# Diagonal scores as column sums of an elementwise product, taken second in the order of the levels

## What is computed

```
g_f = log_forget(h_ff, lb_f); g_b = log_forget(h_fb, lb_b)
k_f = -expm1(g_f); k_b = -expm1(g_b)
out_f = chunk_scan(q, k_f, g_f, v)
out_b = chunk_scan(q[:, ::-1], k_b[:, ::-1], g_b[:, ::-1], v[:, ::-1])[:, ::-1]
o = rmsnorm(out_f + out_b, norm_gain)
...
# inside chunk_scan: b = cumsum(g)
scores = einsum('bhtk,bhsk,bhtsk->bhts', q, k, exp(b_t - b_s))   # s <= t
```

## Time and profile before

| | |
|---|---|
| median of 3 runs | 1738.81 us (1738.01 to 1739.43) |
| the profiled execution's own time | 1739.63 us |
| its span, first to last instruction | 1737.8 us |
| TensorE matmuls busy | 1725.9 us (99%) |
| VectorE busy | 1252.2 us (72%) |
| ScalarE busy | 998.8 us (57%) |
| GpSimd busy | 59.3 us (3%) |
| granted TensorE clock, mean | 0.999 of full |
| moved by DMA | 311.65 MB, 179 GB/s |

### The profile page before, as it was taken

One profiled execution on the slowest core, in us unless ns is written; L12 is line 12 of the kernel. 1 busy time (PEld: TensorE's weight loads), 2 busy tenths in 40 slices (PEclk: granted clock), 3 DMA queues, 4 the chain that ended last, 5 costly groups with the idle time before them and its releaser, 6 DMA issues.

```text
span 1737.8 us, 24185 instructions
## 1 busy us (share of the span) xinstructions
PE 1725.9 (99%) x9517; PEld 1498.4 (86%) x9517; DVE 1252.2 (72%) x1584; ACT 998.8 (57%) x1247; POOL 59.3 (3%) x95
## 2 busy tenths in 40 slices
PE   9999999999999999999999999999999999999998
PEld 8888998888888888888889888888888988888887
DVE  6766777766677566875667898866657898876565
ACT  6544666644467454754457866464446966565454
POOL 7200000000000000000001000000000000000000
PEclk9999999999999999999999999999999999999999
DMA  7765535665655655465545554356565554445652
GB/s 244 240 194 185 177 122 169 217 216 180 206 169 176 206 186 188 141 199 192 193 147 191 186 167 145 122 185 218 178 209 169 164 176 134 138 165 194 200 187 96
DMA packets 211564, 311.65 MB, mean 179 GB/s; under 512 B 6434, under 2 KB 166112, under 8 KB 211360
## 3 DMA queue, kind: packets, MB, share of 16 engines
q1 hardware_dynamic: 207472, 303.84, 53.4%
q0 software_dynamic: 3712, 6.44, 1.3%
q10 hardware_dynamic: 304, 0.33, 0.1%
HBM read 309.54 MB, written 1.05 MB: 179 GB/s over the span
## 4 chain that ended last, share of the span: by engine, by line
PE 90%; ACT 5%; DVE 3%; issue 2%; DMA 0%; SPq 0%; ACTq 0%; DVEq 0%
PE psD L1968 28%; PE psA L1905 20%; PE psA L1912 11%; PE psA L1826 7%; PE psA L1831 3%; PE psA L1935 3%; PE psA L1950 3%; PE psA L1770 3%; PE psA L1968 2%; PE psD L2253 2%; ACT hi L454 2%; PE psA L1954 1%; PE psA L1939 1%; PE psA L1775 1%; PE psA L2038 1%
## 5 line engine op out<-in xcount | busy, mean ns | idle before, releaser
L926 DVE TENSOR_TENSOR lo<-raw,hi 128x2048 fp32r<-128x2048 f32 x285 | 650.6, 2290 | 120.1 <-ACT hi L454 119.4
L454 ACT ACTIVATE hi<-raw 128x2048 fp32r<-128x2048 f32 x285 | 542.9, 1911 | 62.2 <-PE psD L1968 33.5
L1905 PE MATMUL psA<-xT,hi 128*128 128x512 f32 x1536 | 355.9, 389 | 0.0
L1905 PEld LDWEIGHTS psA<-xT,hi 128*128 128x128 f32 x1536 | 288.3, 188 | 59.8
L1968 PE MATMUL psD<-hi,prod_hi 128*128 128x512 f32 x544 | 213.5, 392 | 0.2 <-DVE prod_lo L1303 0.2
L1968 PE MATMUL psD<-hi,prod_lo 128*128 128x512 f32 x544 | 212.6, 391 | 0.0
L592 ACT ACTIVATE scr<-psA 128x512 f32<-128x512 f32 x66 | 39.4, 597 | 296.5 <-PE psA L1912 278.7
L1912 PEld LDWEIGHTS psA<-xT,lo 128*128 128x128 f32 x1536 | 190.6, 192 | 3.7
L1912 PE MATMUL psA<-xT,lo 128*128 128x256 f32 x1536 | 191.8, 283 | 0.0
L1284 DVE TENSOR_TENSOR scr<-psA,scr 128x512 f32<-128x512 f32 x66 | 45.6, 691 | 192.2 <-ACT scr L592 192.2
L1968 PE MATMUL psD<-lo,prod_hi 128*128 128x512 f32 x544 | 143.6, 389 | 0.0
(11 more groups left out here) (311 smaller groups left out, 2155.4 us busy)
## 6 DMA issues: line engine op xcount, KB each, us to landing
raw<-in_w_in SPq DMA_DIRECT2D x48, 1024.0 KB, 5.2
raw<-in_ffn_w_up SPq DMA_DIRECT2D x43, 1024.0 KB, 5.7
raw<-in_ffn_w_gate SPq DMA_DIRECT2D x43, 1024.0 KB, 5.4
raw<-in_ffn_w_down SPq DMA_DIRECT2D x43, 1024.0 KB, 5.0
raw<-in_w_gate SPq DMA_DIRECT2D x22, 1024.0 KB, 5.4
raw<-in_w_up SPq DMA_DIRECT2D x22, 1024.0 KB, 5.6
raw<-in_w_down SPq DMA_DIRECT2D x22, 1024.0 KB, 5.0
raw<-in_lru_w_in SPq DMA_DIRECT2D x10, 1024.0 KB, 5.4
```

The source lines that it names most:

```text
L454: act.activation(hi[:, n % RING, :], raw_of(n), ACT.Copy).then_inc(hi_ready, 1)
L926: dve.tensor_tensor(lo[:, n % RING, :], raw_of(n), hi[:, n % RING, :].bitcast(F32), ALU.subtract).then_inc(lo_ready, 1)
L1905: pe.matmul(psA[:, bank + f, :], w[:, k, f * P:(f + 1) * P], xT[:, k].rearrange("p e s -> p (e s)"), start=(k == 0), stop=False)
```

## The change

The diagonal is no longer a level of its own kind. GpSimd adds the two keys and multiplies the sum by the query, ScalarE and VectorE split the product into a high and a low part (into `prod_hi` and `prod_lo`, which are free at that time), and TensorE multiplies each by a 128x128 tile of ones. Every row of the result then holds the column sums, the diagonal among them. It is made behind block 10, after `pair(0)` and ahead of `pair(1)`.

```
+        ones_r = sb("ones_r", [P, P], F32R)
@@ GpSimd
+                if kind == "mix":
+                    l, HS = stage[1], HEADS * S
+                    pool.wait_ge(kk_ready, 2 * l + 2)
+                    pool.tensor_tensor(view(K_SUM, HS), view(KK, HS), view(KK + HS, HS), ALU.add).then_inc(diag_summed, 1)
+                    pool.wait_ge(diag_summed, l + 1)
+                    pool.wait_ge(query_evac, 2 * l + 2)
+                    pool.tensor_tensor(view(K_SUM, HS), view(K_SUM, HS), view(Q_B, HS), ALU.mult).then_inc(diag_in, 1)
@@ ScalarE
-                        act.wait_ge(pair_done, (NL + 1) * l + i + 2)
+                        act.wait_ge(pair_done, (NL + 1) * l + (2 if i < 0 else 1))
+                    def diagonal_high():
+                        act.wait_ge(diag_in, l + 1)
+                        act.activation(prod_hi[:].rearrange("p a b s -> p (a b s)"), view(K_SUM, HS), ACT.Copy).then_inc(diag_hi, 1)
-                        if i in (E0 + 1, E0 + 3):
-                            take((i - E0 - 3) // 2)
+                        if i == E0 + 2:
+                            diagonal_high()
+                        if i == E0 + 3:
+                            take(0)
+                        if i == E0 + 4:
+                            take(-1)
@@ VectorE
+            settle()
+            dve.tensor_copy(ones_r[:], one_row[:]).then_inc(ones_ready, 1)
-                    def diagonal():
-                        dve.wait_ge(kk_ready, 2 * l + 2)
-                        settle()
-                        dve.tensor_tensor(view(K_SUM, HS), kk2[:, 0:HS], kk2[:, HS:2 * HS], ALU.add).then_inc(scaled_ready, 1)
+                    def diagonal_low():
+                        dve.wait_ge(diag_hi, l + 1)
+                        dve.tensor_tensor(prod_lo[:].rearrange("p a b s -> p (a b s)"), view(K_SUM, HS),
+                                          prod_hi[:].rearrange("p a b s -> p (a b s)").bitcast(F32), ALU.subtract).then_inc(diag_lo, 1)
-                        dve.wait_ge(pair_done, (NL + 1) * l + i + 1)
+                        if i:
+                            dve.wait_ge(pair_done, (NL + 1) * l + (1 if i == 1 else i + 1))
-                            diagonal()
+                                exponents(0)
-                        if (i - E0) % 2 == 0 and l <= (i - E0) // 2 < NL:
+                        if (i - E0) % 2 == 0 and 1 <= (i - E0) // 2 < NL:
+                        if i == E0 + 2:
+                            diagonal_low()
@@ TensorE
+                    def diagonal():
+                        pe.wait_ge(ones_ready, 1)
+                        pe.wait_ge(diag_lo, l + 1)
+                        pe.wait_ge(pair_taken, (NL + 1) * l + 1)
+                        for b in range(2):
+                            for z in (prod_hi, prod_lo):
+                                last = pe.matmul(psD[:, b, :], ones_r[:], z[:, b].rearrange("p a s -> p (a s)"), start=(z is prod_hi), stop=(z is prod_lo))
+                        last.then_inc(pair_done, 1)
-                        if (i - E0) % 2 == 0 and 0 <= (i - E0) // 2 < NL:
+                        if (i - E0) % 2 == 0 and 0 < (i - E0) // 2 < NL:
                             pair((i - E0) // 2 - 1)
+                        if i == E0 + 3:
+                            diagonal()
```

More of the change, by code:

```diff
@@ L176, in build @@
         scaled_ready, pair_done, pair_taken = sem("scaled_ready"), sem("pair_done"), sem("pair_taken")
+        diag_summed, diag_in, diag_hi, diag_lo, ones_ready = sem("diag_summed"), sem("diag_in"), sem("diag_hi"), sem("diag_lo"), sem("ones_ready")
         rec_done, rec_square, rec_sum, rec_rms, rec_ready = sem("rec_done"), sem("rec_square"), sem("rec_sum"), sem("rec_rms"), sem("rec_ready")
@@ L2238, in _ @@
                     qkT, w_att, wT = view(QK_T, 2, HEADS, S), view(W_ATT, 2, S), view(W_T, 2, T, P)
-                    def pair(i):
[L2242 to L2248, removed]
+                    def diagonal():
[6 more added lines that the diff above has]
+                        last.then_inc(pair_done, 1)
+                    def pair(i):
+                        pe.wait_ge(scaled_ready, NL * l + i + 1)
+                        if i:
+                            pe.wait_ge(pair_taken, (NL + 1) * l + i + 1)
+                        q, k_ = tmp2[:, 0], tmp2[:, 1]
                         ps = psD[:, 0:2, :].rearrange("p b (e s) -> p (b e) s", s=P)
@@ L2251, in pair @@
                             for e in range(T):
-                                te = 1 - e if i >= 0 and LEVELS[i] == P else e
+                                te = 1 - e if LEVELS[i] == P else e
                                 last = pe.matmul(ps[:, 2 * hh + e, :], k_[:, hh, e * P:(e + 1) * P], q[:, hh, te * P:(te + 1) * P],
```

## The result

The changed kernel takes 1743.42 us (median of 9 runs, 1741.92 to 1744.83) against 1738.73 us before (9 runs, 1738.00 to 1739.43): a ratio of 1.0027, 95% interval 1.0017 to 1.0037. It is slower by 4.7 us, where 1.6 us were forecast, and it lies outside the forecast range, which ended at 1742.4. Its runs are also spread twice as wide as those of before, 2.9 against 1.4 us. The profiled execution took 1743.6 us with a span of 1741.8 us, 4.0 us more than the span of before.

The account below looks back on a forecast made before the run. The prediction took TensorE to bound the kernel. Layer 0's +1.5 us and layer 1's +0.1 us sum to 1.6 us, giving 1740.4 us on the median 1738.81; the range was 1737.4 to 1742.4 us.

Parts of the forecast that it names:

- VectorE is held in layer 0: Layer 0: GpSimd's addition holds block 7's low part 0.57 us, its product costs VectorE some 2.3 us; layer +1.5 us.
- The product of GpSimd was itself held: Layer 0: GpSimd's second instruction would itself have to wait while VectorE makes a low part; otherwise about 2 us sooner.
- The wait ahead of block 8's low matmuls: Layer 0: TensorE wants block 8's low part at 983.0, waits till 985.75, and goes on 1.05 us later than before.
- `pair(0)` without a wait: Layer 0: scaled operands are ready when TensorE arrives, so the earlier 0.47 us wait goes; start at 993.0 against 992.43.
- Layer 1: Second layer: GpSimd adds beside VectorE work with one SBUF operand, its product holds block 7's low part; sum +0.1 us.
- late low part: Layer 1, block 7: low part done at 1375.8, wanted at 1374.99; TensorE waits 0.85 us, at no cost.
- the wait for the bank: Layer 1, middle of block 8: TensorE waits for ScalarE to empty a bank until 1381.76, about 1.2 us.
- The cast stands at the very start: Kernel start, VectorE: making the ones takes some 0.2 us that nobody waits for.
- The matmuls by ones: TensorE, each layer: four matmuls of 512 columns add 0.92 us, bounds 0.9 and 1.2 us.
- the moved copies: ScalarE: added copy falls in idle time, `take(-1)` moves behind second `turn_heads`; no cost, up to 1 us a layer if uncovered.
- VectorE's rotation: Layer 1, second `rotate`: with the subtraction (1.14 us) ahead of it, done 0.1 us later than TensorE comes for it.
- slower than can be overlooked: Rival, layer 0: GpSimd's instructions last longer beside busy VectorE or written in place; with 3.6 us, 1742.7 us; chance 0.07.

## Why the prediction was wrong

**That VectorE is held in layer 0: right.** From one row I took a price of 2.9 us for low part and scans; it was 0.5 + 2.2. The product of GpSimd was itself held, as I took it. The wait ahead of block 8's low matmuls, the place of it, and `pair(0)` without a wait came as said.

**The failing step is "Layer 1", first sentence:** GpSimd adds "while VectorE has work with one SBUF operand". I knew one kind of blocking and took its absence for safety. Nearly all of that work is tensor_scalar, and these are held too, as the run with memsets shows even by an instruction that only writes. They were longer by 3.9 us. The forecast's late low part was 0.85 us and swallowed by the wait for the bank; it was 2.8 and stood well above it. Layer 1 lost 1.65 us more than forecast. The section of the Trainium skill that the prediction cites ("SBUF — State Buffer", "Who interferes with whom") names this operation too, a few lines further on. The trace of before gives no more than a hint. Four of VectorE's tensor_scalar with 512 columns:

```profile
960.40 1.67 DVE L1060 TENSOR_SCALAR h<-scr,stat 128x512 f32<-128x512 f32 x4
```

That is 0.4 us from start to start, where an instruction with two SBUF operands and 512 columns takes 0.6 (926.80 to 927.44). So tensor_scalar is not simply a tensor_tensor with one operand fewer. But the eight that were held show nothing of the kind: with 256 columns they took 0.32 us from start to start, between the 0.2 us of a tensor_tensor of 128 columns and the 0.6 of 512. From their length I could not have told.

**The missing term is the clock.** I priced a wait at its length. Behind waits of 2.3 to 2.9 us TensorE's clock fell in five of the eight cases that the profiles hold, which in the changed kernel's cost 1.76 us more; behind the 0.5 us waits of before it did not. Filling the waits gave 1.4 us back.

**"The cast stands at the very start, where VectorE waits for data; some 0.2 us": wrong** by the same rule as in layer 1, 6.22 us. How much of that reaches the time was not resolved.

**The rest was right in size.** The matmuls by ones took 0.93 us in layer 0 (forecast 0.92); in layer 1 `turn_heads` began 1.17 us behind their start, the rest being a wait for VectorE's rotation, which is 0.1 us longer than before, as forecast. TensorE waited nowhere for the moved copies. The wait for the bank in layer 1 I had in the wrong place: the first bank, which I took as free, was emptied at 1379.38 in the profile before, and without `pair(-1)` block 8 would want it at 1378.63. In the run without GpSimd's instructions `turn_heads` of layer 0 comes 1.26 us sooner relative to block 6 (forecast 1.25) and that of layer 1 0.14 us later (forecast 0.1). The runs split the loss into -0.8 (all but GpSimd) + 3.0 (layer 0) + 2.7 (layer 1) = 4.9 us. These are successive differences, so that the sum comes out is no check; it differs from the measured 4.7 only by the two medians of before. The rival "slower than can be overlooked" had the sign and a false mechanism: GpSimd's instructions kept their 2.40 us of work, and only the product of layer 0 lasted longer, because it waited. So the direction was forecast for a good reason, and the size missed for two others.

## What to carry to other kernels

An idle GpSimd is not free: here its elementwise instructions took VectorE's time as well, when VectorE then had an instruction with two SBUF operands or a tensor_scalar, and its memset held a cast. Before work is moved there, list every VectorE instruction that will run beside it by both rules, not by one. And a wait of TensorE as long as these can cost more than its length; where it can't be removed, try matmuls that nobody reads, which here gained 1.4 us.

## What was not expected of the hardware

- A tensor_scalar of 256 float32 columns with one SBUF tensor waits for GpSimd, whether that reads and writes (6.57 us for eight) or only writes (6.64 us), against 2.67 us alone. GpSimd's instruction was not held by it (2.40 us).
- A cast of 128 columns beside GpSimd's memset of 7680 columns took 6.22 us; alone 0.22 us.
- The reverse holds too: GpSimd's product waited 1.9 us for a VectorE low part that ran first (4.34 us for 2.40 of work).
- The fall of the clock behind a wait of 2.3 to 2.9 us is not certain. In the changed kernel's profile it came behind the 2.3 us wait and not behind the 2.8 us one; in the run with the first filled it came behind the second. In the one profile of each run that has them, it came behind five of eight such waits. A wait of 1.4 us was followed by 1.00.
